# Half of a table of experts through a dense matrix: the last stage of a two-block model rebuilt

## The reference

```python
def block(hb):                                   # 128 tokens
    q = (hb @ w_query).reshape(PEER_BLOCK, PEER_HEADS, 2, D_KEY // 2)
    s = jnp.einsum('thpc,hpnc->thpn', q, sub_keys)
    top_s, top_i = lax.top_k(s, PEER_TOPK)       # 16 of 128, twice a head
    cand_s = top_s[:, :, 0, :, None] + top_s[:, :, 1, None, :]
    cand_i = top_i[:, :, 0, :, None] * N_KEYS + top_i[:, :, 1, None, :]
    best_s, best_j = lax.top_k(cand_s, PEER_TOPK)          # per head
    idx = take_along_axis(cand_i, best_j)
    g = softmax(best_s)
    a = gelu(einsum('thkd,td->thk', u[idx], hb))
    return einsum('thk,thkd->td', g * a, v[idx])
```

## Time and profile before

| | us |
|---|---|
| median of 3 runs (lowest, highest) | 3404.21 (3401.13, 3404.91) |
| span of the profiled execution | 3402.5 |
| around the span, to the median | 1.7 |
| first dot product of the experts' stage | 2134.3 |
| TensorE busy in the span | 2507.2 |
| VectorE busy | 1781.8 |
| ScalarE busy | 1081.7 |
| GpSimd busy | 2364.1 |

### The profile page before, as it was taken

How to read it: one execution, slowest core, us unless ns; L and a number is a source line. 1 busy time by engine, 2 the same in 40 slices (tenths; PEclk the granted TensorE clock), 3 DMA queues, 4 the chain that set the end, 5 groups by cost and what they waited for, 6 DMA issues and landing times.

```text
span 3402.5 us, 42238 instructions
## 1 busy us (share of the span) xinstructions
PE 2507.2 (74%) x15833; PEld 1974.7 (58%) x15833; DVE 1781.8 (52%) x2456; ACT 1081.7 (32%) x2108; POOL 2364.1 (69%) x1677
## 2 busy tenths in 40 slices
PE   7999996989999999989999899108503730571077
PEld 5777885779988998889988679103201310230032
DVE  4375656242200223220412446997797879778954
ACT  6444424464444444454546554000000100000000
POOL 7400316859999999987866579886687578568853
PEclk9999997999999999999999999559856965796589
DMA  5684300546655665555544346999999999999998
GB/s 180 206 237 145 105 3 26 185 123 183 185 191 187 183 183 185 187 153 161 161 131 125 117 164 206 396 427 427 427 428 427 427 427 427 428 426 427 427 427 344
DMA packets 241376, 868.10 MB, mean 255 GB/s; under 512 B 18940, under 2 KB 21484, under 8 KB 174886
## 3 DMA queue, kind: packets, MB, share of 16 engines
q0 software_dynamic: 73776, 536.97, 37.5%
q1 hardware_dynamic: 163414, 316.11, 30.6%
q10 hardware_dynamic: 4016, 12.75, 1.3%
HBM read 860.24 MB, written 2.10 MB: 253 GB/s over the span
## 4 chain that ended last, share of the span: by engine, by line
PE 50%; POOL 19%; DMA 11%; DVE 7%; issue 4%; ACT 1%; DVEq 0%; ACTq 0%; POOLq 0%; SPq 0%
PE acc L2022 20%; PE acc L2032 19%; DMA zone<-in_peer_v,zone 10%; POOL lasting L736 10%; POOL zone L736 9%; PE acc L2028 3%; PE acc L2160 3%; PE acc L2586 2%; POOL w_lo L616 1%; DVE lasting L1962 1%; DMA lasting<-in_peer_u,zone 1%; PE acc L2475 1%; DVE zone L1568 0%; PE acc L2069 0%; DVE x_lo L1697 0%
## 5 line engine op out<-in xcount | busy, mean ns | idle before, releaser
L616 POOL TENSOR_TENSOR w_lo<-lasting,w_hi 128x512 fp32r<-128x512 f32 x1024 | 1372.4, 1359 | 276.0 <-ACT w_hi L785 257.3
L785 ACT ACTIVATE w_hi<-lasting 128x512 fp32r<-128x512 f32 (+1 forms) x1184 | 741.3, 631 | 903.6 <-PE acc L2022 457.0
L2586 PE MATMUL acc<-zone,lasting 128*128 128x512 f32 x512 | 256.3, 655 | 694.3 <-ACT lasting L1297 643.4
L2586 PEld LDWEIGHTS acc<-zone,lasting 128*128 128x128 f32 x512 | 105.2, 210 | 841.6 <-ACT lasting L1297 505.2
L2032 PE MATMUL acc<-x_hi,w_hi 128*128 128x256 f32 (+1 forms) x1856 | 305.5, 286 | 11.5 <-DVE x_lo L1697 4.3
L736 POOL DMA_INDIRECT zone<-in_peer_v,zone x128 | 192.2, 1502 | 165.6 <-DVE lasting L1962 73.6
L1932 DVE CUSTOM_DVE_ANT_0 zone<-zone 128x2048 f32<-128x2048 f32 x128 | 293.4, 2292 | 21.9 <-DMA zone<-in_peer_u,zone 7.1
L1932 DVE CUSTOM_DVE_ANT_0 zone<-lasting,zone 128x2048 f32<-128x2048 f32 x128 | 293.5, 2293 | 21.0 <-DMA lasting<-in_peer_u,zone 8.6
L2032 PE MATMUL acc<-x_lo,w_hi 128*128 128x256 f32 (+1 forms) x1856 | 298.6, 283 | 0.0
L2032 PE MATMUL acc<-x_hi,w_lo 128*128 128x256 f32 (+1 forms) x1856 | 298.3, 283 | 0.0
L2586 PE MATMUL acc<-lasting 128*128 128x512 f32 x512 | 247.8, 635 | 64.9 <-DMA zone<-in_peer_v,zone 38.2
(11 more groups left out here) (419 smaller groups left out, 3951.7 us busy)
## 6 DMA issues: line engine op xcount, KB each, us to landing
lasting<-in_w_in SPq DMA_DIRECT2D x200, 512.0 KB, 3.7
lasting<-in_w_up SPq DMA_DIRECT2D x128, 512.0 KB, 3.8
lasting<-in_w_down SPq DMA_DIRECT2D x128, 512.0 KB, 3.6
lasting<-in_w_mix_out SPq DMA_DIRECT2D x32, 512.0 KB, 3.6
lasting<-in_w_out SPq DMA_DIRECT2D x32, 512.0 KB, 3.6
lasting<-in_peer_w_query SPq DMA_DIRECT2D x32, 512.0 KB, 3.7
lasting<-in_w_kv_cross SPq DMA_DIRECT2D x16, 512.0 KB, 3.7
lasting<-in_w_q_cross SPq DMA_DIRECT2D x8, 512.0 KB, 3.7
```

The costliest lines, as they stand in the source:

```text
L616: pool.tensor_tensor(w_lo[:, k, 0:width], ring[:, slot, s % SLOT_SLABS, 0:width], w_hi[:, k, 0:width].bitcast(FP32), ALU.subtract).then_in ...
L785: act.activation(w_hi[:, s % PARTS, 0:width], ring[:, slot, s % SLOT_SLABS, 0:width], ACT.Copy).then_inc(hi_ready, 1)
L2586: last = pe.matmul(bank(4 * t + c), diag[:, n // 2, k], rows_buf[2 * n + k][:, c * CHUNK:(c + 1) * CHUNK], start=hx % 2 == 0 and i == 0 an ...
```

## The change

U is used as before: one gather of full rows per slot (`gather_u`), 16 buffers at first, 14 from slot 16 on and 7 for the second tile, one dot product per gather. The order of `choose` and `coefs` among the 256 dot products is written out (`CHOOSE_AFTER`, `COEFS_AFTER`); three calls of `choose` come before the first of them, among these one of the second tile.

V is split by columns. Columns 1024 to 2047 are still gathered, by half rows of 4 KB (`gather_v`, four buffers), one per slot. The first 72 of them (`V_EARLY`) are issued between the U gathers 80 to 151 and weighed by PE with diagonals; the other 184 are issued after all U gathers and weighed by DVE, 16 of them one behind each second group of one-hots.

Columns 0 to 1023 are no longer gathered. A matrix `dense[t]` [128 keys, 128 keys, 128 tokens] holds a token's coefficient at each expert it chose, and PE multiplies it with all of V, 128 experts a product. The matrix is built from one-hots: for each token two 128x128 matrices (slot by first key, and slot by second key times the coefficient) whose fp32 product is that token's slice; four tokens make a group. ACT builds the one-hots of tile 0 (with Abs, Relu and Copy), DVE those of tile 1; ACT copies both from PSUM. SP loads V in tiles of 128 experts x 1024 columns, 512 KB (`V_LOADS`): 36 for tile 0 alone before tile 1's matrix is begun, 11 beside its groups, then the same 47 again for tile 1, then the remaining 81 for both tiles.

Lines that are left out here are memory places, names of semaphores, the removed bodies and the transposes of keys and coefficients.

```diff
+        U_SPOTS = [base + 4096, base + 6144, half_rows_at, half_rows_at + D, free_row_at] + [n * D for n in range(4)]
+        U_SPOTS += [X0 + n * D for n in range(4)] + [C_AT + TILES * P * N_KEYS // 2, base, base + D]
+        U_SPOTS += [scores_at, scores_at + D, hb_at]
+        u_rows = [at(spot, D) for spot in U_SPOTS]
+        FIRST_TILE, SECOND_TILE = (5, 7, 8, 13, 4, 6, 0, 1, 9, 10, 11, 12, 14, 15), (5, 7, 8, 13, 4, 16, 18)
+        U_SLOTS = TILES * P
+        U_BUF = [q if q < 16 else FIRST_TILE[(q - 16) % 14] if q < P else SECOND_TILE[(q - P) % 7] for q in range(U_SLOTS)]
+        U_SEM = [b if b < 16 else b - 7 for b in U_BUF]
+        U_USE = [U_SEM[:q].count(U_SEM[q]) for q in range(U_SLOTS)]
+        U_BEFORE = [max([k for k in range(q) if U_SEM[k] == U_SEM[q]], default=None) for q in range(U_SLOTS)]
+        half_rows = [at(half_rows_at + n * HALF_D, HALF_D) for n in range(4)]
+        V_EARLY = 72
+        V_AFTER = {80 + k: k for k in range(V_EARLY)}
+        CHOICES = [(0, 0), (0, 1), (1, 0), (0, 2), (0, 3), (1, 1), (1, 2), (1, 3)]
+        CHOSEN = {choice: n + 1 for n, choice in enumerate(CHOICES)}
+        CHOOSE_AFTER = dict(zip((32, 56, 140, 168, 198), CHOICES[3:]))
+        COEFS_AFTER = {66: 0, 129: 1, 220: 2, 255: 3}
+        HALF_ROWS = P // 2
...
+        dense = [x.rearrange("p (i s) -> p i s", s=P) for x in (dense0, dense1)]
+        GROUPS = TILES * P // 4
+        one_hot = at(D, 2, 2 * 4 * P)
+        hot_of = lambda g, k: one_hot[:, g % 2, k * 4 * P:(k + 1) * 4 * P].rearrange("p (n c) -> p n c", n=4)
+        V_SPOTS = [X0, 0, HALF_D, 2 * D, 5 * HALF_D, 3 * D, 7 * HALF_D]
+        ALONE_BEFORE, ALONE_BESIDE = 36, 11
+        ALONE = ALONE_BEFORE + ALONE_BESIDE
+        V_LOADS = [(i, (0,)) for i in range(ALONE)] + [(i, (1,)) for i in range(ALONE)] + [(i, (0, 1)) for i in range(ALONE, N_KEYS)]
+        spot_of = lambda n: (n - ALONE_BEFORE) % len(V_SPOTS)
+        v_tile = lambda n: half_rows[n % 4] if n < ALONE_BEFORE else at(V_SPOTS[spot_of(n)], HALF_D)
...
+            for n, (i, tiles) in enumerate(V_LOADS):
+                if n == 0:
+                    sp.wait_ge(s_wpe, V_EARLY)
+                if n == ALONE_BEFORE:
+                    sp.wait_ge(s_dot, 2 * TILES)
+                if 4 <= n < ALONE_BEFORE:
+                    sp.wait_ge(slab_used, v_used(n - 4))
+                elif n >= ALONE_BEFORE + len(V_SPOTS):
+                    sp.wait_ge(slab_used, v_used(n - len(V_SPOTS)))
+                if n >= 4:
+                    sp.wait_ge(*v_landed(n - 4))
+                sp.dma_start(v_tile(n), A["peer_v_2"][0][i * P:(i + 1) * P, 0:HALF_D]).then_inc(v_landed(n)[0], 16)
...
+            def gather_u(q):
+
+                t, j, b = q // P, q % P, U_BUF[q]
+                if j % 32 == 0:
+                    pool.wait_ge(s_ix0, CHOSEN[t, j // 32])
+                if U_USE[q]:
+                    pool.wait_ge(s_dotted, U_BEFORE[q] + 1)
+                if b == 16:
+                    pool.wait_ge(s_ix0, CHOSEN[0, 3])
+                elif b == 18:
+                    pool.wait_ge(s_dot, 2)
                 pool.indirect_dma_start(
-                    out=rows_buf[2 * n + k], out_offset=None, in_=A[table][0],
-                    in_offset=bass.IndirectOffsetOnAxis(ap=experts[:, hx // 2, j:j + 1], axis=0)
-                ).then_inc(rows_full[n], 16)
-
-            early = [(0, 0), (0, 1), (1, 0), (1, 1), (2, 0)]
-            rests("query", after={at_: lambda n=n, k=k: gather(0, 0, n, k) for at_, (n, k) in zip(((2, 15), (3, 2), (3, 5), (3, 8), (3, 11)), early)})
+                    out=u_rows[b], out_offset=None, in_=A["peer_u_2"][0],
+                    in_offset=bass.IndirectOffsetOnAxis(ap=experts[:, t, j:j + 1], axis=0)
+                ).then_inc(u_full[U_SEM[q]], 16)
+
+            v_halves = A["peer_v_2"][0].rearrange("e (c d) -> (e c) d", c=2)
+
+            def gather_v(q):
+
+                t, j, b = q // P, q % P, q % 4
+                if q >= V_EARLY + 4:
+                    pool.wait_ge(s_wdve, q - 4 - V_EARLY + 1)
+                elif q >= V_EARLY:
+                    pool.wait_ge(slab_used, v_used(ALONE_BEFORE - 4 + q - V_EARLY))
+                elif q >= 4:
+                    pool.wait_ge(s_wpe, q - 4 + 1)
+                else:
+                    pool.wait_ge(s_dotted, 4)
+                pool.indirect_dma_start(
+                    out=half_rows[b], out_offset=None, in_=v_halves,
+                    in_offset=bass.IndirectOffsetOnAxis(ap=half_rows_no[:, t, j:j + 1], axis=0)
+                ).then_inc(v_full[b], 16)
...
+                gather_u(q)
+                if q in V_AFTER:
+                    gather_v(V_AFTER[q])
+            for q in range(V_EARLY, U_SLOTS):
+                gather_v(q)
...
+            def one_hots(g):
+
+                if g >= 2:
+                    act.wait_ge(s_dense, g - 1)
+                for n in range(4):
+                    s_ = 4 * g + n
+                    for k in range(2):
+                        last = act.activation(hot_of(g, k)[:, n], key_no, ACT.Abs, scale=-1.0, bias=keysT[:, k, s_:s_ + 1])
+                step(last)
+                step(act.activation(one_hot[:, g % 2], one_hot[:, g % 2], ACT.Relu, scale=-1.0, bias=1.0))
+                for n in range(4):
+                    s_ = 4 * g + n
+                    last = act.activation(hot_of(g, 1)[:, n], hot_of(g, 1)[:, n], ACT.Copy, scale=coefT[:, 0, s_:s_ + 1])
+                last.then_inc(s_hot, 1)
...
+            exp_gates(0)
+            gelu_dots(0)
+            exp_gates(1)
+            act.wait_ge(s_coefs, 1)
+            for q in range(48):
+                diagonal(q)
+            gelu_dots(1)
+            for q in range(48, V_EARLY):
+                if q == P // 2:
+                    act.wait_ge(s_coefs, 2)
+                diagonal(q)
+            exp_gates(2)
+            read_keys(0)
+            read_coefs(0)
+            for g in range(GROUPS // TILES):
+                one_hots(g)
+                if g:
+                    read_dense(g - 1)
+            read_dense(GROUPS // TILES - 1)
+            exp_gates(3)
+            gelu_dots(2)
+            read_keys(1)
+            gelu_dots(3)
+            read_coefs(1)
+            for g in range(GROUPS // TILES, GROUPS):
+                read_dense(g)
...
-            def dot_products(hx):
...
-            def weigh_rows(hx, i):
...
-            def add_sums(t):
...
+            def one_hots(g):
+
+                dve.wait_ge(s_dense, g - 1)
+                for n in range(4):
+                    s_ = 4 * (g - GROUPS // TILES) + n
+                    TS(hot_of(g, 0)[:, n], key_no, keysT[:, 2, s_:s_ + 1], None, ALU.is_equal)
+                    last = TS(hot_of(g, 1)[:, n], key_no, keysT[:, 3, s_:s_ + 1], coefT[:, 1, s_:s_ + 1], ALU.is_equal, ALU.mult)
+                last.then_inc(s_hot, 1)
+
+            def weigh_half_row(q):
+
+                t, j, b = q // P, q % P, q % 4
+                dve.wait_ge(v_full[b], half_landed(q))
+                STT(h[:, t, HALF_D:], half_rows[b], coef[:, t, j:j + 1], h[:, t, HALF_D:], ALU.mult, ALU.add).then_inc(s_wdve, 1)
...
+            for t, c in CHOICES[:3]:
+                dve.wait_ge(s_sc, c + 1)
+                choose(t, c)
+            dve.wait_ge(lo_ready, G["query"].slab(0, 3, SLABS - 1) + 1)
+            for q in range(U_SLOTS):
+                dot_product(q)
+                if q % HALF_ROWS == HALF_ROWS - 1:
+                    dve.nop().then_inc(s_dot, 1)
+                if q in CHOOSE_AFTER:
+                    t, c = CHOOSE_AFTER[q]
+                    if t == 0:
+                        dve.wait_ge(s_sc, c + 1)
+                    choose(t, c)
+                    if c == 3:
+                        split_experts(t)
+                if q in COEFS_AFTER:
+                    coefs(COEFS_AFTER[q])
+            dve.wait_ge(s_keysR, 2)
+            dve.wait_ge(s_coefR, 2)
+            done = V_EARLY
+            for g in range(GROUPS // TILES, GROUPS):
+                one_hots(g)
+                if g % 2:
+                    weigh_half_row(done)
+                    done += 1
+            dve.wait_ge(s_wpe, V_EARLY)
             for c in range(2):
-                dve.wait_ge(s_sc, c + 1)
-                choose(0, c)
-            dve.wait_ge(lo_ready, G["query"].slab(0, 3, SLABS - 1) + 1)
-            for hx in range(2 * TILES):
-                dot_products(hx)
-                coefs(hx)
-                for i in range(ROUNDS):
-                    weigh_rows(hx, i)
-                    if i < 2 and hx + 1 < 2 * TILES:
-                        t, c = (hx + 1) // 2, (hx + 1) % 2 * 2 + i
-                        if t == 0:
-                            dve.wait_ge(s_sc, c + 1)
-                        choose(t, c)
-                    if i == 2 and hx == 2:
-                        add_sums(0)
-            add_sums(1)
+                add_bank(0, 2 + c, 4 + c)
+                dve.drain()
```

(52 more changed lines are left out.)

209 lines of the change are left out of this document (106 added, 103 removed).

## The result

The changed kernel takes 3470.99 us (median of 4 runs, 3467.09 to 3473.55), the kernel before, on the same chip, 3404.51 (3401.13 to 3404.91). The ratio is 1.0199, with a 95% interval of 1.0185 to 1.0213: 2% slower. I had forecast 3440, range 3375 to 3495, slower by 1%. The direction and the map of the stages came out; 31 us of size did not: 3471 lies outside the range of my main case, 3425 to 3455, and inside the whole range only because that was widened for slower rivals, none of which happened.

A forecast was written before the change was run, and what follows sets the result against it. The last stage was taken to be bound by DMA bytes at 427 GB/s. Bytes saved 72 us, holes gave back 126, some 20 us was slack at the old end: 3438 us of span, 3440 median, range 3375 to 3495.

The forecast's parts named there:

- main case: Whole kernel: slower, 3425 to 3455 us, around a forecast of 3440; chance 0.35.
- slower rivals: ScalarE's building as the bound (3471 us) or a slower gather queue (3450 to 3503); together 0.25.
- Start, stage A: First dot product at 2153; then U gathers 0 to 79, VectorE-bound to 2354, 37 us of DMA lost.
- Bytes: Transfers of the last stage: 42.5 MB less; at 1.29 us a half transfer, 72 us saved, not 99.
- the rival of the slower queue: 4 KB packets at 1.36 us, pairs staying at 4.84: 3450 to 3503; 0.25 together with ScalarE's building as bound.
- Stage B: 72 pairs of U gather and V half gather: 12 at 4.84 us, 60 at 3.75; last half row about 2646.
- ScalarE's build: First dense matrix: 5.7 us a group, 182 us in all, to 2835, covered by 20 us before coefs(2).
- The rival with ScalarE as the bound: First dense matrix at 7.5 us a group delays VectorE: 31 us more, 3471; 0.25 together with the slower queue.
- Stages C and D: Rest of U: VectorE-bound to 2838, 30-odd us of DMA lost, then shared with 32 loads; U ends at 2975.
- Stage E: Second dense matrix, by VectorE: 2.15 us a group, 69 us, between 50 and 88; 20 us of transfers lost.
- Stage F: Remaining loads and gathers: queues take turns, loads every 2.58 us for tile 1 alone; 381 us against TensorE's 358.
- the engines keep up with both queues: Rest of U and last loads: loads cost gathers nothing, 49 us off, 3391; 0.24 including better outcomes.

The follow-up runs named there:

- the buffers in turn: Changed kernel with only the order in which the first tile's gathers reuse the row buffers altered, the buffer of dot product 0 first: 3475.44 us, 1.0215.
- The choices in pairs: Changed kernel with all four calls of choose for tile 1 put behind dot products 82, 96, 110 and 124: 3434.57 us, 1.0104.

## Why the prediction was right in direction and short in size

The span came out 32.6 us above my 3438.

- **Start, stage A.** 2150.85 and 2352.8 against 2153 and 2354. The loss, 0.18 of 202 us, is 36 against my 37. Shown by the halved dot products and by the buffers in turn. The dozen rows that VectorE stood behind were there too: its first wait for a row came at 2410.5, and I had 2412.
- **Bytes.** My 1.29 us for a half transfer was too high where the engines are full. In D one row of U and one load, 1.573 MB, come every 3.7 us, 425 GB/s; in F a load and a gather every 2.50, so 1.25 each. That also refutes the rival of the slower queue, with its 1.36 and its pairs at 4.84. The Trainium skill's 408.7 GB/s for a load stream of 4 KiB rows ("DMA: Bandwidth & Descriptors", iDMA vs SDMA table) is below what these windows show where only 4 KB rows move, 418 to 420.
- **Stage B** ended at 2648 (2646), the pairs at 3.7 us.
- **ScalarE's build** took 5.22 us a group, not 5.7 (no gaps between dependent steps), and was over at 2818 for 2835. VectorE reached coefs(2) at 2874, so 54 us of cover, not 20. The rival with ScalarE as the bound is dead, although its 3471 is the number that was measured: the time agreed, the mechanism did not.
- **Stages C and D: +6 by the start of E** (2988.0 for 2982). I let VectorE run without a gap through C. It idled 16.5 us there, and not where I would have looked for it: 10 of them lie before 2672, where the DMA share is 1.01 and the rows simply come no faster; behind the two calls of choose it hardly waits. The hole of the DMA engines is the calls themselves, in the windows from 2700 and from 2790:

```profile
2648.00:2670.00 22.00, 7.51 (x30) 6.09 (x29) 12.38 (x11) 20.82 (x58) 11.91 (x10) 0.59 1.01 406
...
2700.00:2730.00 30.00, 12.45 (x48) 10.68 (x48) 28.06 (x68) 29.64 (x84) 9.77 (x5) 0.50 0.60 244
...
2790.00:2819.00 29.00, 12.60 (x49) 10.83 (x49) 26.88 (x75) 26.97 (x74) 7.88 (x5) 0.50 0.42 170
```

  VectorE's last dot product of U ended 11 us late; turning the columns took 2 us in place of 7. The choices in pairs showed that the hole is real (344 to 426 GB/s).
- **Stage E: +19, the term that was most mis-sized.** 88 us, not 69. I took 0.175 us for a 128x128 one-hot, between 0.10 and 0.25; it is 0.228, near the upper bound. That is 1.82 a group for 1.4, 13 us over 32 groups. The half row adds 1.37 for 1.35. The other 5 us are VectorE's waits for TensorE's groups (3.5 us before L2096) and the last group's way to the matrix: 5 us from the last one-hot (3071.0) to its read at 3076.05, against 2 us in three other runs. The granted clock was 0.68 in the last 11 us of the stage here (eight records of a group's product took 2.07 us and not 1.16) and 1.00 there, where E took 83 to 84 us; so some 4 of the 19 belong to this one execution. The hole of the DMA engines in E is 36 us (0.41 of 88), and I had 20.
- **Stage F: +8, the mechanism right.** 389 us for 381. The turn-taking is there: 36 loads every 2.50 us while tile 1 is alone, and I had 2.58. It goes with the Trainium skill's rule of round-robin between queues ("DMA: Bandwidth & Descriptors", queues, rings and completion order), and the trace agrees, one to one in each 2.51 us. What I had too low is the start of the part: 40 x 2.58 lets loads arrive from its first microsecond, but all seven buffers were full then, and a new load waits for one to be freed. 11 loads went at TensorE's pace in 20 us, 36 came at 2.50 in 90: 110 us (3076.7 to 3186.9) for 103. The loads for both tiles took 278, as forecast, and "the other 124 gathers fit" came out as well, with 12.8 us to spare.
- **Its reason did not hold, which cost the experiments.** I priced the gathers by their bytes, 1.29 us. Each of four buffers goes round through the wait for the gather to be issued, its landing, and 1.28 us of weighing, so that a half row takes 1.9 us with nothing beside it and 2.2 beside the loads for both tiles (123 in the 266 us from 3186.9). In the changed kernel that chain is 12.8 us short of being the end, so it cost nothing there; the 31 us above TensorE's 358 are the turns. Reordering the loads gains nothing and halving the products gains nothing, since then the chain or the turns elsewhere set the end; removing the gathers, which takes away both, gains 27 us; and two more buffers gain 14 and 30.
- **The rival "the engines keep up with both queues"** (0.24 with the better ones) was wrong at both its places: D ran at the rate of the bytes, and F lost to the turns.

What stays open: which part of a gather's round, its issue, its descriptors or its landing, sets the chain; what makes the smaller hole in B when the choices stand there in pairs; and why moving one call of choose gave 10 us of its 18.8. Six buffers were as many as found room, so more was not tried.

## What to carry to other kernels

Fewer bytes pay only where the queue stays full. Before was one steady stream behind 16 buffers; the change cuts 8% of its bytes, but puts VectorE's long steps, the calls of choose and the one-hots, where few buffers cover them. Price a ring of few buffers as a latency loop (buffers over round trip), not by its bytes. And when two chains end within some 13 us of each other, an experiment that shortens one alone shows little: here only removing the gathers, or giving them more buffers, moved the end of F.
